# Modulation sums of four vectors in one total on 32 partitions each, read out by one selector product

## The chip, the cores and the metric

One Trainium2 chip, one of its cores. The metric is device time in microseconds (us) of one execution of the whole kernel; the number given is the median of several executions.

## The reference, cut to what matters

Two transformer blocks run on a sequence of 256 positions of width 1024, batch 1, all in fp32. The first has two layers: a convolution mixer and a recurrent/attention mixer, each followed by a gated feed-forward network (FFN) with a 3-tap causal convolution. The second has two layers of FFN, pooling/attention mixer, FFN, each with a modulation that comes from a vector `c` of 1024 numbers:

```python
D_MODEL, SEQ, DEPTH, D_FF, N_SUBLAYERS = 1024, 256, 2, 2816, 3

def modulate(h, shift, scale):
    return h * (1 + scale[:, None, :]) + shift[:, None, :]

# inputs: c (1, 1024); ada_w (2, 1024, 9*1024); ada_b (2, 9*1024)
...
        h = modulate(rms_norm(x, ffn2_norm[l]), sh3, sc3)
        x = x + 0.5 * g3[:, None, :] * swiglu(h, ffn2_w_gate[l], ffn2_w_up[l], ffn2_w_down[l])
```

The nine modulation vectors of a layer (shift, scale and gate of three sublayers, each 1024 wide) are silu(c) @ ada_w[l] + ada_b[l], so there are 18 vectors in the two layers. Each is a product of one row of 1024 with a 1024 x 1024 matrix, 4 MB of weights.

## The kernel before, in words

**Layout.** The activations stand with their 1024 features on 128 partitions in eight tiles. Every weight is split into a high part (ScalarE, line 1078, `wh`) and a low part (VectorE, line 1507, `wl`, the function `lo`), and TensorE multiplies high by high, high by low and low by high. Weights come as units of 1 MB into three slots (`raw`), in one fixed order that SP's queue issues (line 466). A unit's load waits until the split of the unit three places before is done. There are three slots of high and low parts as well.

**An FFN** (ffn0 and ffn1 with convolution, then fa0, fb0, fa1, fb1 without) is eleven blocks of three units: a gate unit, an up unit and, for the block before, a down unit (TensorE lines 666/667 and 768). A block takes TensorE some 17 us. VectorE's part of a block (`part` in its `ffn`) is, in order: the first addition into the gate columns (line 1632), in the convolution FFNs four tap instructions (1641), the split of the next gate unit, the second addition (1654), the product with the activation (1663), the split of the next up unit, the low part of the product (1672, `FX`), the split of the next down unit. Between them ScalarE copies from PSUM (1144, 1169), applies the first tap (1150) and the activation (1164), and makes the high parts (1177). Blocks 2 and later run in a loop of two blocks an iteration; the last ones are written out.

**The modulation sums** run inside five of these FFNs. VectorE does them as multiply-adds: a step takes 128 rows of one vector's matrix (128 x 1024, 512 KB, loaded by one DMA at line 482 into a ring of four slots `ada`), multiplies each row by its number of silu(c), which stands in a column of `CA`, and adds it to the vector's total of 128 x 1024 in `Z` (line 1606; the first step of a vector has no total to add to and is line 1603). A vector needs 8 steps; a block holds four: after the gate split, after the up split, and two after the down split. `ADA_SUMS` says how many vectors an FFN sums: 4, 3, 4, 3, 4 in ffn0, ffn1, fa0, fb0 and fa1, each in its own total and in as many loop iterations as vectors. A load's issue waits until the step four before has been done (`ada_sum`).

**The selector products.** A total still has to be summed over its 128 partitions. `ada_sum_rows` does this on TensorE: for each vector and each half of 512 columns one fp32 product with a 128 x 4 selector from `pick`, whose one column of ones puts the sum into row v of a PSUM bank (line 694). ScalarE copies the four rows out (1098, `ada_take`), TensorE turns them (702, `ada_turn`), VectorE adds the biases (1515, `ada_read`). It happens at five places (`ADA_GAP`): "od" after the fourth unit of the second mixer, in front of its gate matmuls (941, 942) that wait for convolution taps (1944, 1947); "fa0" and "fa1" at the start of these FFNs, in front of the first unit; "w0" and "w1" in the pooling/attention mixers, in front of the q product, whose operand's low part is line 2069.

**Around it.** `angles` is a chain of small VectorE instructions (1749 to 1764) that runs once, in ffn1, before the first addition of block 9. Parameters (gains, biases, taps, `c`) are loaded at the start as rows of `AR` by SP (528, 532), between the first weight units; TensorE turns them in `NPG` groups (882), VectorE copies them out (1816).

## Time and profile before

| | |
|---|---|
| median of 3 executions | 1613.81 us (1613.39 to 1614.95) |
| profiled execution, own time | 1613.69 us |
| its span | 1611.7 us |
| TensorE busy | 1589.0 us (99%) |
| VectorE busy | 1262.0 us (78%) |
| ScalarE busy | 855.1 us (53%) |
| GpSimd busy | 58.6 us (4%) |
| granted TensorE clock, mean | 0.999 |
| HBM read | 341.32 MB |

A line such as `L1606 DVE ...` is line 1606 of the kernel on VectorE; PE is TensorE (PEld its weight loads, PEq its sequencer), ACT ScalarE, POOL GpSimd, SP SyncE, whose work is issuing DMAs. Times in a timeline count from the start of the span. A time in brackets is how long the engine stood idle before the instruction, with the instruction that released it. A matmul's recorded time overlaps the next one's, so matmuls are paced by their starts or by the chain.

### The profile page before, as it was taken

The numbers are of one execution on the slowest core, as the hardware profiler recorded it, in microseconds if no ns is written. First come the engines' busy times: TensorE is split into PE (matmuls) and PEld (weight loads), VectorE is DVE, ScalarE is ACT, GpSimd is POOL, SyncE is SP. The second block draws the span as 40 slices with busy tenths as digits, with TensorE's granted clock in tenths as the row PEclk, the third lists the DMA queues.
The fourth block names the chain that finished last, engine by engine and source line by source line (L and its number), as shares of the span: only waits on it lengthen the run. The fifth ranks groups of instructions, "written<-read, shape, count | busy, mean of one in ns | idle before, by whom it ended". The sixth has DMA issues, their size and how long they took to land.

```text
span 1611.7 us, 26970 instructions
## 1 busy us (share of the span) xinstructions
PE 1589.0 (99%) x11042; PEld 1451.2 (90%) x11044; DVE 1262.0 (78%) x1447; ACT 855.1 (53%) x1025; POOL 58.6 (4%) x76
## 2 busy tenths in 40 slices
PE   9999999999999999999999999999999999999998
PEld 8989999988898999899998899999899998899997
DVE  7978889877678997878878697885878887785555
ACT  6566555555465545644446474445544455564443
POOL 3001000000010000000000010000000000010000
PEclk9999999999999999999999999999999999999999
DMA  9414988644238885498864349875598854265552
GB/s 266 162 53 161 349 300 304 217 158 147 79 119 299 299 290 180 146 325 310 314 216 135 112 158 329 314 243 183 173 324 301 308 167 160 93 196 183 185 194 76
DMA packets 231438, 343.48 MB, mean 213 GB/s; under 512 B 7066, under 2 KB 194048, under 8 KB 231360
## 3 DMA queue, kind: packets, MB, share of 16 engines
q1 hardware_dynamic: 230304, 340.94, 62.4%
q0 software_dynamic: 752, 1.18, 0.2%
q8 instruction: 55, 0.90, 0.2%
q10 hardware_dynamic: 304, 0.27, 0.1%
q14 instruction: 23, 0.19, 0.0%
HBM read 341.32 MB, written 1.05 MB: 212 GB/s over the span
## 4 chain that ended last, share of the span: by engine, by line
PE 80%; DVE 10%; issue 6%; ACT 3%; DMA 0%; DVEq 0%; ACTq 0%
PE PS L666 21%; PE PS L768 19%; PE PS L667 11%; PE PS L657 9%; PE PS L635 5%; PE PS L738 3%; DVE wl L1507 3%; PE PS L644 3%; PE PS L694 2%; PE PS L905 2%; ACT wh L1078 1%; DVE XL L1523 1%; DVE Z L1606 1%; PE PS L832 1%; PE PS L854 1%
## 5 line engine op out<-in xcount | busy, mean ns | idle before, releaser
L1507 DVE TENSOR_TENSOR wl<-raw,wh 128x2048 fp32r<-128x2048 f32 (+2 forms) x256 | 570.1, 2229 | 147.3 <-ACT wh L1078 145.3
L666 PE MATMUL PS<-HP,wh 128*128 128x512 f32 x1728 | 608.0, 395 | 2.1 <-DVE wl L1507 2.1
L1078 ACT ACTIVATE wh<-raw 128x2048 fp32r<-128x2048 f32 (+2 forms) x256 | 475.5, 1859 | 134.0 <-PE PS L768 114.9
L667 PE MATMUL PS<-HP,wl 128*128 128x256 f32 x1728 | 484.6, 280 | 0.0
L666 PEld LDWEIGHTS PS<-HP,wh 128*128 128x128 f32 x1728 | 324.0, 188 | 76.7 <-DVE wl L1507 2.5
L768 PE MATMUL PS<-FX,wh 128*128 128x256 f32 x1920 | 345.0, 281 | 0.4 <-DVE FX L1672 0.4
L667 PEld LDWEIGHTS PS<-HP,wl 128*128 128x128 f32 x1728 | 326.5, 189 | 0.0
L768 PEld LDWEIGHTS PS<-FX,wh 128*128 128x128 f32 x1920 | 294.5, 188 | 2.9 <-issue 0.6
L768 PE MATMUL PS<-FX,wl 128*128 128x256 f32 x960 | 269.9, 281 | 0.0
L768 PEld LDWEIGHTS PS<-FX,wl 128*128 128x128 f32 x960 | 180.4, 188 | 0.0
L1606 DVE SCALAR_TENSOR_TENSOR Z<-ada,CA,Z 128x1024 f32 x126 | 161.4, 1281 | 1.3
L635 PE MATMUL PS<-FX,wh 128*128 128x258 f32 (+2 forms) x592 | 145.0, 285 | 4.7 <-DVE BI L1628 1.8
L635 PE MATMUL PS<-FX,wl 128*128 128x258 f32 (+2 forms) x592 | 143.7, 282 | 0.0
L657 PE MATMUL PS<-HP,wh 128*128 128x256 f32 x768 | 140.9, 285 | 1.2 <-ACT HP L1111 0.6
L1144 ACT ACTIVATE WK<-PS 128x512 f32<-128x512 f32 x54 | 32.3, 598 | 196.8 <-PE PS L667 196.8
L657 PEld LDWEIGHTS PS<-HP,wh 128*128 128x128 f32 x768 | 119.8, 192 | 7.3 <-issue 2.6
L635 PEld LDWEIGHTS PS<-FX,wh 128*128 128x128 f32 (+1 forms) x592 | 111.1, 188 | 8.7 <-DVE BI L1628 2.2
L635 PEld LDWEIGHTS PS<-FX,wl 128*128 128x128 f32 (+1 forms) x592 | 111.2, 188 | 0.0
L657 PE MATMUL PS<-HP,wl 128*128 128x256 f32 x384 | 107.5, 283 | 0.0
L1169 ACT ACTIVATE WK<-PS 128x512 f32<-128x512 f32 x54 | 32.0, 593 | 97.1 <-PE PS L667 97.1
L644 PE MATMUL PS<-XL,wh 128*128 128x256 f32 (+1 forms) x592 | 77.5, 282 | 0.0
L657 PEld LDWEIGHTS PS<-HP,wl 128*128 128x128 f32 x384 | 73.6, 192 | 0.0
(286 smaller groups left out, 1752.7 us busy)
## 6 DMA issues: line engine op xcount, KB each, us to landing
ada<-ada_w SPq DMA_DIRECT2D x144, 512.0 KB, 6.0
raw<-ffn_w_gate SPq DMA_DIRECT2D x66, 1024.0 KB, 5.4
raw<-ffn_w_up SPq DMA_DIRECT2D x66, 1024.0 KB, 5.4
raw<-ffn_w_down SPq DMA_DIRECT2D x66, 1024.0 KB, 5.0
raw<-od_w_in SPq DMA_DIRECT2D x13, 1024.0 KB, 5.3
raw<-ev_w_in SPq DMA_DIRECT2D x10, 1024.0 KB, 8.1
raw<-w_in SPq DMA_DIRECT2D x8, 1024.0 KB, 5.4
raw<-w_out SPq DMA_DIRECT2D x8, 1024.0 KB, 5.8
```

Of the source, the lines that this page charges most:

```text
L635: mm(bank(dst + m, 0, width, slice(0, rows[m])), lhsT=w(a, k, m * P, rows[m]), rhs=XH[:, k, 0:width], start=k == 0 and a == 0, stop=False, ...
L644: last = mm(bank(dst + m, 0, S, slice(0, rows[m])), lhsT=w(0, k, m * P, rows[m]), rhs=XL[:, k, :], start=False, stop=k == KD - 1, skip_gro ...
L657: last = mm(dst, lhsT=lhs(a, k), rhs=rhs(b, k), start=first and i == 0, stop=first and i == len(order) - 1, skip_group_check=not first)
L666: mm(pairs(bank(bk)), lhsT=lhs(0, k), rhs=HP[:, k], start=k == 0, stop=False, skip_group_check=True)
L667: last = mm(bank(bk, 0, S), lhsT=lhs(1, k), rhs=HH[:, k, :], start=False, stop=k == k_tiles - 1, skip_group_check=True)
L694: last = mm(bank(bk + h, 0, 512, slice(0, 4)), lhsT=cn("pick")[:, 3 - v:7 - v], rhs=Z[:, at + v * D + 512 * h:at + v * D + 512 * h + 512], ...
L738: last = mm(bank(bk, m * S, S), lhsT=w(a, k, m * P, P), rhs=H[b][:, k, :], start=m == 0 and k == 0 and i == 0, stop=False, skip_group_chec ...
L768: last = mm(bank(m // 2, (m % 2) * S, S), lhsT=w(a, k, m * P, P), rhs=rhs(b, k), start=begins and i == 0 and m % 2 == 0, stop=False, skip_ ...
L1078: last = A_(dst(wh), src, ACT.Copy)
L1144: A_(pairs(E), PS[:, 4:6, S:], ACT.Copy).then_inc(g_copy, 1)
L1507: last = tt(dst(wl), src, dst(wh).bitcast(F32), ALU.subtract)
L1606: ins = stt(total, w, CA[:, k:k + 1], total, ALU.mult, ALU.add)
```

## The change

Four vectors share one total. Partitions 32i to 32i+31 of the total belong to vector i of the group. A step's slot of `ada` is filled by four DMAs, each 32 rows of one vector's matrix into 32 partitions, so 32 steps sum the four vectors (16 steps sum a group of two, on 64 partitions each). The total is 128 x 1024 for the whole group. VectorE clears it first, and then every step is a multiply-add (the form without a total is gone); its coefficient is a column of `CA`, chosen by a register, which now holds silu(c) in two layouts: 32 columns for 32 rows repeated four times, 16 columns for 64 rows repeated twice. These come from `c` by four and two parameter loads in the place of one, and the parameters fill six groups instead of five. The selector has four columns of ones, one for each quarter (or half), so that one product per half of the columns sums all vectors of the group: two products at each of the five places. The groups are 4, 4, 4, 4 and 2, so ffn1 and fb0 sum four vectors where they summed three, and fa1 two where it summed four. `angles` moves from before block 9 to before block 10 of ffn1, since the loop now covers block 9.

```diff
--- before.py
+++ after.py
@@ -64,7 +64,8 @@
     r.append(("lba", "od_lru_ba", (0,), 4))
     r.append(("lbx", "od_lru_bx", (0,), 4))
     r.append(("lam", "od_lru_lam", (0,), 4))
-    r.append(("c", "c_2", (), 8))
+    r.append(("c4", "c_2", (), 32))
+    r.append(("c2", "c_2", (), 16))
     r.append(("qng", "od_q_norm_g", (0,), 1))
     r.append(("kng", "od_k_norm_g", (0,), 1))
     r.append(("cfw", "ev_cf_conv_w", (0,), 124))
@@ -110,7 +111,7 @@
 def const_layout():
     at = 0
     for name, n in (("ident", P), ("ones", P), ("freq", 1), ("eps", 1), ("mask", 3 * P), ("identb", P // 2), ("heads", 22), ("rot", P),
-                    ("cmask", 2 * P), ("krdup", P), ("krrot", P), ("pick", 7), ("edge", 4 * 16)):
+                    ("cmask", 2 * P), ("krdup", P), ("krrot", P), ("pick", 8), ("edge", 4 * 16)):
         CONST[name] = (at, n)
         at += n
     return at
@@ -167,8 +168,9 @@
     put("edge", e)
     inv = (np.float32(1.0) / np.power(np.float32(10000.0), np.arange(0, 64, 2, dtype=np.float32) / np.float32(64))).astype(np.float32)
     put("freq", np.tile(inv, 4)[:, None])
-    pk = np.zeros((P, 7), np.float32)
-    pk[:, 3] = 1.0
+    pk = np.zeros((P, 8), np.float32)
+    for i in range(P):
+        pk[i, i // 32] = pk[i, 4 + i // 64] = 1.0
     put("pick", pk)
     put("eps", np.full((P, 1), EPS, np.float32))
     return c
@@ -238,8 +240,8 @@
     _n += SUM_PARTS.get(_name, 3)
 
 
-ADA_SUMS = {"ffn0": 4, "ffn1": 3, "fa0": 4, "fb0": 3, "fa1": 4}
-ADA_GAP = {"od": 4, "fa0": 3, "w0": 4, "fa1": 3, "w1": 4}
+ADA_SUMS = {"ffn0": 4, "ffn1": 4, "fa0": 4, "fb0": 4, "fa1": 2}
+ADA_GAP = {"od": 4, "fa0": 4, "w0": 4, "fa1": 4, "w1": 2}
 AC_AT = {"ffn0": 0, "ffn1": 0, "fa0": 1536, "fb0": 0, "fa1": 1536}
 ADA_FROM = dict(zip(ADA_GAP, ADA_SUMS))
 ADA, ADA_AT, _a = {}, {}, 0
@@ -249,7 +251,8 @@
     _a += _k
 assert _a == N_ADA
 
-N_PAR = len(param_rows()) + 2
+COPIES = {"qng": 2, "kng": 2, "c4": 4, "c2": 2}
+N_PAR = sum(COPIES.get(e[0], 1) for e in param_rows())
 TWO_PI = 6.283185307179586
 
 
@@ -301,7 +304,7 @@
         CN = sb("CN", [P, NCONST])
         GM = sb("GM", [P, 6, KD])
         HG = sb("HG", [P, 4, KD])
-        CA = sb("CA", [P, KD])
+        CA = sb("CA", [P, 48])
         SM = sb("SM", [P, 48])
         COS = sb("COS", [P, S])
         SIN = sb("SIN", [P, S])
@@ -472,14 +475,17 @@
                     c = min(256, width - 256 * pair)
                     load(n0 + i, w[:, :, 256 * pair:256 * pair + c], lambda s: s.rearrange("p (k n) -> p k n", k=k))
 
-            aw = A["ada_w_2"].rearrange("l (k p) n -> p l k n", p=P)
-
-            def load_ada(step):
-                g, k = divmod(step, KD)
+            aw = A["ada_w_2"]
+
+            def load_ada(step, at, n):
+
                 if step >= ADA_RING:
-                    sp.wait_ge(ada_sum, step - ADA_RING + 1)
-                l, v = divmod(g, N_ADA // 2)
-                sp.dma_start(ada[:, step % ADA_RING], aw[:, l, k, v * D:(v + 1) * D]).then_inc(ada_in[step % ADA_RING], 16)
+                    sp.wait_ge(ada_sum, step - ADA_RING + 2)
+                for i in range(4):
+                    l, v = divmod(at + i * n // 4, N_ADA // 2)
+                    r = (step - KD * at) * (P // n) + (0 if n == 4 else 32 * (i % 2))
+                    sp.dma_start(ada[32 * i:32 * i + 32, step % ADA_RING],
+                                 aw[l, r:r + 32, v * D:(v + 1) * D]).then_inc(ada_in[step % ADA_RING], 16)
 
             def load_ffn(name, gate, up, down):
                 n0 = U0[name]
@@ -495,7 +501,7 @@
                 def ada_part(j, *ks):
                     if name in ADA_AT and 2 <= j <= 2 * ADA_SUMS[name] + 1:
                         for k in ks:
-                            load_ada(KD * ADA_AT[name] + 4 * (j - 2) + k)
+                            load_ada(KD * ADA_AT[name] + 4 * (j - 2) + k, ADA_AT[name], ADA_SUMS[name])
 
                 wide(n0, gate, 0)
                 wide(n0 + 1, up, 0)
@@ -523,9 +529,10 @@
                 for at in index:
                     v = v[at]
                 dst = AR[r:r + rows, g * P:(g + 1) * P]
-                if name in ("qng", "kng"):
-                    for h in range(2):
-                        sp.dma_start(dst[:, 64 * h:64 * h + 64], v.unsqueeze(0)).then_inc(par_in, 16)
+                if name in COPIES:
+                    m = P // COPIES[name]
+                    for h in range(COPIES[name]):
+                        sp.dma_start(dst[:, m * h:m * h + m], v.rearrange("(t p) -> t p", p=m)).then_inc(par_in, 16)
                     continue
                 if len(v.shape) == 2:
                     v = v.rearrange("k c -> (k c)")
@@ -688,11 +695,11 @@
                 n, at = ADA_GAP[name], AC_AT[ADA_FROM[name]]
                 if ADA[name]:
                     pe.wait_ge(ada_out, ADA[name])
-                pe.wait_ge(ada_sum, KD * (ADA[name] + n))
+                pe.wait_ge(ada_sum, KD * (ADA[name] + n) + 1)
+                pick = cn("pick")[:, 0:4] if n == 4 else cn("pick")[:, 4:8]
                 for h in range(2):
-                    for v in range(n):
-                        last = mm(bank(bk + h, 0, 512, slice(0, 4)), lhsT=cn("pick")[:, 3 - v:7 - v],
-                                  rhs=Z[:, at + v * D + 512 * h:at + v * D + 512 * h + 512], start=v == 0, stop=v == n - 1)
+                    last = mm(bank(bk + h, 0, 512, slice(0, 4)), lhsT=pick, rhs=Z[:, at + 512 * h:at + 512 * h + 512],
+                              start=True, stop=True)
                 last.then_inc(ada_rows, 1)
 
             def ada_turn(name, bk):
@@ -1288,7 +1295,8 @@
             act.wait_ge(ev("ln_var"), 1)
             A_(RT[:, 0:S], bank(7, 0, S), ACT.Sqrt, scale=1.0 / CF, bias=cn("eps")).then_inc(ev("ln_root"), 1)
             act.wait_ge(ev("par_out"), NPG)
-            A_(CA[:], pc("c", 0, 8), ACT.Silu).then_inc(ev("silu_c"), 1)
+            A_(CA[:, 0:32], pc("c4", 0, 32), ACT.Silu).then_inc(ev("silu_c"), 1)
+            A_(CA[:, 32:48], pc("c2", 0, 16), ACT.Silu).then_inc(ev("silu_c"), 1)
             act.wait_ge(ev("ln_normed"), 1)
             for t in range(4):
                 A_(T[:, 4 + t, :], cols(Z, EV["A"], 4)[:, t, :], ACT.Silu, scale=pc("lng", t),
@@ -1594,17 +1602,15 @@
                 lo(n0 + 5)
                 raw_lo(name, 2, gain)
 
-            def ada_step(at, at_z, off, k):
-
+            def ada_step(name, off, k):
+
+                at, at_z, n = ADA_AT[name], AC_AT[name], ADA_SUMS[name]
                 step = KD * at + k
-                dve.wait_ge(ada_in[k % ADA_RING], 16 * (step // ADA_RING + 1) + 16 * (KD // ADA_RING) * off)
-                total, w = Z[:, bass.ds(off * D + at_z, D)], ada[:, k % ADA_RING]
-                if k == 0:
-                    ins = ts(total, w, CA[:, 0:1], None, ALU.mult)
-                else:
-                    dve.wait_ge(ada_sum, KD * off + step)
-                    ins = stt(total, w, CA[:, k:k + 1], total, ALU.mult, ALU.add)
-                ins.then_inc(ada_sum, 1)
+                dve.wait_ge(ada_in[k % ADA_RING], 64 * (step // ADA_RING + 1) + 64 * (KD // ADA_RING) * off)
+                total, w = Z[:, at_z:at_z + D], ada[:, k % ADA_RING]
+                dve.wait_ge(ada_sum, KD * off + step + 1)
+                c = CA[:, bass.ds(KD * off + (0 if n == 4 else 32) + k, 1)]
+                stt(total, w, c, total, ALU.mult, ALU.add).then_inc(ada_sum, 1)
 
             def ffn(f, name, gain, gate=None, chain=None, at_end=None):
                 n0, fb, conv = U0[FFNS[f]], f * NFB, f < 2
@@ -1614,7 +1620,7 @@
                 def part(j, par, ng, nu, nd, off=0, ks=(), mid=None):
                     def ada_some(i):
                         for k in ks[i]:
-                            ada_step(ADA_AT[FFNS[f]], AC_AT[FFNS[f]], off, k)
+                            ada_step(FFNS[f], off, k)
 
                     ks = ks or ((), (), ())
                     C = WK[:, par * 512:(par + 1) * 512]
@@ -1683,11 +1689,17 @@
                 part(1, 1, n0 + 2, n0 + 3, n0 + 4)
                 steps = [((4 * b,), (4 * b + 1,), (4 * b + 2, 4 * b + 3)) if sums else () for b in range(2)]
                 n = sums or 3
+                if sums:
+                    zero = dve.memset(Z[:, AC_AT[FFNS[f]]:AC_AT[FFNS[f]] + D], 0.0)
+                    if f == 0:
+                        zero.then_inc(ada_sum, 1)
+                    else:
+                        own.link(zero)
                 with dve.Fori(0, n) as i:
                     for b in range(2):
                         part(2 * i + (2 + b), b, n0 + 5 + 3 * b, n0 + 6 + 3 * b, n0 + 7 + 3 * b, i, steps[b])
                 for j in range(2 * n + 2, NFB):
-                    if f == 1 and j == 9:
+                    if f == 1 and j == 10:
                         angles()
                     part(j, j % 2, n0 - 1 + 3 * j, n0 + 3 * j, n0 + 1 + 3 * j if j + 1 < NFB else None)
                 if at_end is not None:
@@ -1913,7 +1925,7 @@
             ffnn0, mixn1, ffnn1 = lambda t: pc("ffnn0", t), lambda t: pc("mixn1", t), lambda t: pc("ffnn1", t)
             out_units(U0["ev_out"], "ffn0", ffnn0)
             chain = norm("ffn0", ffnn0, deferred=U0["ffn0"] + 2)
-            dve.wait_ge(ev("silu_c"), 1)
+            dve.wait_ge(ev("silu_c"), 2)
             ffn(0, "mix1", mixn1, chain=chain)
```

## Rows read from the trace of the kernel before

**Rows 1.** Page, part 1.
```profile
PE 1589.0 (99%) x11042; PEld 1451.2 (90%) x11044; DVE 1262.0 (78%) x1447; ACT 855.1 (53%) x1025; POOL 58.6 (4%) x76
```

**Rows 2.** Groups by line (xcount, busy us, mean ns), then the chain: selector products.
```profile
L694 PE MATMUL PS<-Z,CN 128*4 128x512 f32 x72 | 31.7, 592 | 0.0
...
344.33 6.96 PE PS L694 x16
```

**Rows 3.** Timeline, VectorE, od gap (start us, us, instruction).
```profile
348.83 3.25 DVE L1947 SCALAR_TENSOR_TENSOR T<-Z,PR,T 128x256 f32<-128x256 f32 x8
```

**Rows 4.** Timeline, ScalarE, fa0 gap ([idle before <-releaser]).
```profile
657.01 1.02 ACT L1098 ACTIVATE AR<-PS 4x1024 f32<-4x1024 f32 x1 [2.34 <-PE PS L694]
```

**Rows 5.** Timeline, VectorE and TensorE, w0 gap.
```profile
882.45 1.49 DVE L2069 TENSOR_TENSOR HP<-Z,HP 128x1280 fp32r<-128x1280 f32 x1 [1.34 <-ACT HP L1430]
...
893.26 2.29 DVE L1507 TENSOR_TENSOR wl<-raw,wh 128x2048 fp32r<-128x2048 f32 x1 [2.82 <-ACT wh L1078]
...
902.72 2.05 PE L832 MATMUL PS<-Z 128*128 128x128 f32 x16 [0.35 <-DVE Z L2102]
```

**Rows 6.** Timeline of ffn0, then down units of fb1 in the chain.
```profile
165.85 0.69 DVE L1632 TENSOR_TENSOR WK<-PS,WK 128x512 f32<-128x512 f32 x1 [0.31 <-ACT WK L1144]
...
178.51 2.29 DVE L1507 TENSOR_TENSOR wl<-raw,wh 128x2048 fp32r<-128x2048 f32 x1 [0.43 <-ACT wh L1078]
...
234.87 0.68 DVE L1632 TENSOR_TENSOR WK<-PS,WK 128x512 f32<-128x512 f32 x1
...
303.35 0.68 DVE L1632 TENSOR_TENSOR WK<-PS,WK 128x512 f32<-128x512 f32 x1
...
312.24 0.47 PE L768 MATMUL PS<-FX,wh 128*128 128x256 f32 x2 [0.44 <-DVE FX L1672]
...
1456.71 5.76 PE PS L768 x48
...
1490.54 5.76 PE PS L768 x48
```

**Rows 7.** VectorE: groups by line, then timeline (memset; fa0).
```profile
L1606 DVE SCALAR_TENSOR_TENSOR Z<-ada,CA,Z 128x1024 f32 x126 | 161.4, 1281 | 1.3
...
L1603 DVE TENSOR_SCALAR Z<-ada,CA 128x1024 f32 x18 | 13.5, 748 | 0.0
...
329.59 0.27 DVE L1923 MEMSET RS<- 128x256 f32 x1
...
729.94 2.29 DVE L1507 TENSOR_TENSOR wl<-raw,wh 128x2048 fp32r<-128x2048 f32 x1 [0.80 <-ACT wh L1078]
```

**Rows 8.** Timeline, VectorE, ffn1, then its last down units in the chain.
```profile
603.59 0.68 DVE L1632 TENSOR_TENSOR WK<-PS,WK 128x512 f32<-128x512 f32 x1
...
616.66 0.28 DVE L1749 CAST WK<-SIN 128x256 f32<-128x256 int32 x1
...
621.39 0.69 DVE L1632 TENSOR_TENSOR WK<-PS,WK 128x512 f32<-128x512 f32 x1
...
640.52 11.21 PE PS L768 x96
```

**Rows 9.** DMA in ffn0 (40 slices), issues with landing, timeline of fa0.
```profile
GB/s 386 414 357 58 19 0 0 0 0 108 96 248 361 376 390 386 405 424 386 371 268 219 304 373 381 369 359 427 369 417 405 395 424 395 424 414 405 405 424 415
...
raw<-ffn_w_up SPq DMA_DIRECT2D x66, 1024.0 KB, 5.4
...
720.88 0.38 SPq L466 DMA_DIRECT2D raw<-ffn_w_up  x1
...
733.57 1.91 ACT L1078 ACTIVATE wh<-raw 128x2048 fp32r<-128x2048 f32 x1
```

**Rows 10.** Table by stretch: us, busy by engine, granted clock, DMA, GB/s.
```profile
1607.00:1608.00 1.00, 0.00 (x0) 0.00 (x0) 0.96 (x3) 1.00 (x3) 0.00 (x0) 0.77 0.00 0
```

**Rows 11.** Timeline, VectorE, even mixer.
```profile
77.23 2.29 DVE L1507 TENSOR_TENSOR wl<-raw,wh 128x2048 fp32r<-128x2048 f32 x1 [2.59 <-ACT wh L1078]
```

**Rows 12.** DMA rate, 10 to 27 us in 40 slices.
```profile
GB/s 347 349 347 347 352 345 345 352 345 352 349 347 350 367 384 446 395 338 268 300 330 279 265 349 406 294 182 159 149 147 122 127 172 222 253 287 294 311 277 241
```

## The prediction

> **What bounds the kernel now.** I read the page first: TensorE is busy 99% of the span, VectorE 78% [rows 1]. A saving counts only if TensorE really reaches its next work sooner; a delay counts once it reaches TensorE. The groups of instructions and the chain give the work that the change removes: 72 records of the selector products, two to a product, in five places, of which one stands [rows 2]. Third come the timelines around these places, to see what waits there already, and the two paces of a feed-forward (FFN) block. TensorE alone needs 33.83 us for two blocks (1456.71 to 1490.54), but in ffn0 the first additions of blocks 6 and 10 are 68.48 us apart (234.87 to 303.35), 34.24 for two blocks, with no idle time before them: that is VectorE's own cycle [rows 6]. VectorE falls behind there by 0.4 us per two blocks, and at the end of ffn0 TensorE already waits 0.44 us for it. Last comes DMA: in one block with sums it rests for only about 3.4 us of 17 [rows 9].
>
> **Selector products, by place.** A product takes 0.87 us (16 records in 6.96 us), so the five places fall from 8, 6, 8, 6 and 8 products to 2 each: 26 x 0.87 = 22.6 us of TensorE work gone. Only part of it is path.
> - od: the next matmul needs convolution taps that VectorE ends between 350.9 and 352.1, four tiles at 0.4 us each; TensorE came at 351.3 [rows 2, 3]. It now comes 5.2 us earlier and waits: gain 0.3 of 5.2.
> - fa0, fa1: ScalarE had been idle for 2.34 us when the rows came at 657.0, so it takes them as soon as TensorE has them [rows 4]. Nothing else is late: gain 3.4 each.
> - w0, w1: 6 products are 5.2 us, but the low part of the next operand is ready at 883.9, so TensorE arriving at 882.1 waits until 884.0 instead of starting at 887.4: 3.4. VectorE had idled 2.82 us before its split at 893.26; with the high part 3.3 us earlier it is late by the other 0.5, and TensorE waits for VectorE at 902.72 already: 2.9 each [rows 5].
> Sum: 0.3 + 6.8 + 5.8 = **12.9 us gained**.
>
> **VectorE, ffn0.** The first step of each vector becomes a multiply-add: 1.28 for 0.75 us, 0.53 more, once in two blocks. The clear of the total is added; a 256-wide memset is 0.27 us and a 1024-wide tensor_scalar 0.75, so I take 0.72 (bounds 0.27 and 1.28). In ffn0 the clear meets an idle 0.31 before block 2's first addition and the lag an idle 0.43 at 178.5: 0.72 + 0.53 - 0.31 - 0.43 = 0.5 us after the first two blocks, then 3 x 0.53: 2.1 us in all. Nothing absorbs it, as the last down unit already waits [rows 6, 7]: **2.1 us lost**. The register arithmetic moves from the total to the coefficient; I cost it at nothing, as the queue can do it under the instruction before; the tap instructions take a coefficient from a register already.
>
> **VectorE, ffn1.** It goes from three pairs of blocks with sums to four, and the angle chain moves from before block 9 to before block 10. Before, blocks 8 to 10 without sums let VectorE recover. After, the first addition of block 10 comes at 603.59 + 1.56 (lag) + 34.24 + 0.53 + 4.73 (angles: 616.66 to 621.39) = 644.65 us. ffn0 shows 8.89 us from that addition to the last down unit (303.35 to 312.24), so 653.5; TensorE is free for it at 646.1 (640.52 plus half of 11.21): **7.4 us lost** [rows 6, 8]. Queued behind the angles are the last block's additions, taps, the split of the last unit and the product that TensorE needs.
>
> fb0 gets eight steps more and fa1 sixteen fewer; without convolution VectorE idles 0.80 us before a split [rows 7], and 0.53 fits: nothing.
>
> **Clock.** At the end of the kernel TensorE has no work left, and in 1607 to 1608 the granted clock averages 0.77: it falls there from 2.4 to 1.2 GHz [rows 10]. A wait of 7 us would see that too. Its price lies between nothing and a down unit at 1.2 GHz throughout, 5.6 us; I take 1, as one short stretch is hit.
>
> **Start.** Five more parameter loads stand on SP's queue before a weight load, at no more than the 0.38 us of a weight load's issue, 1.9 us; VectorE idles 2.59 us at 77 us, which takes that up [rows 9, 11]. One transpose more: 0.1 us.
>
> **The loads.** Each 512 KB load becomes four, each into 32 partitions. SP issues four where it issued one, at 0.38 us or less each, 1.5 us; its next weight load waits for a split 4 us and more later: hidden. The transfer itself is what the trace doesn't show. While data flows in a block with sums (204 to 221 us), it moves about 395 GB/s; the 5.24 MB of a block need 13.3 us, 5.3 of them for the 2.10 MB of the vectors [rows 9]. One bound is that narrow loads cost the same, or less. The nearest row for loads into few partitions is the start, where the small parameter loads run: 122 to 182 GB/s between 21 and 25 us, against 345 to 352 with wide ones [rows 12]; their packets are also small, so it is the outer bound (0.4 of the rate). I take half the rate, between the two but nearer to the only narrow row: 10.6 us for the vectors, 18.6 for the block. The block lasts 17.4 with convolution, 16.9 without. The queue lags by 1.2 and 1.7 us per block, plus 1.7 at once, as a down unit with two vector loads outlasts its gap. Against it stands the lead of the weights: an up unit issued at 720.88 lands 5.4 us later and is read at 733.57, 7.3 after that [rows 9]; I take the same for the convolution FFNs. Over 8 blocks: 9.6 + 1.7 - 7.3 = 4.0 us twice (ffn0, ffn1) and 13.6 + 1.7 - 7.3 = 8.0 twice (fa0, fb0); fa1 has 4 blocks and stays within its lead. **24.0 us lost** (bounds 0 and, at 0.4 of the rate, where a block takes 21.2 us and fa1 stalls too, about 119).
> The Trainium skill (SBUF — State Buffer, Door 1: The DMA port swizzle) says that a load's bandwidth depends on how many of 16 ports its partitions reach, and that 32 neighbouring partitions reach 8. By it the vectors' loads run at half rate, which is also my figure; by its advice to use one load over all partitions the change is the wrong way round. No row here shows it.
>
> **Sum.** 1613.7 (the profiled execution's own time, 2.0 over its span and 0.1 under the median) - 12.9 + 2.1 + 7.4 + 1.0 + 0.1 + 24.0 = 1635.4, say **1635 us**.
>
> **Rivals.**
> - A, not slower: the narrow loads stay hidden. For it: DMA rests 3.4 us a block, and small packets alone may explain the start's rate. Then 1611.4; it decides at a flow for the vectors above about 230 GB/s, where the block takes 17.1 us. Between 1609 and 1614. Chance 0.33.
> - B, all of the selector products pay: fillers can be taken away where other work is ready. The rows at od and w0 speak against it. With the loads hidden and VectorE's lag absorbed: 1613.7 - 22.6 + 0.7 = about 1592. Chance 0.04.
> - C, the loads are worse than half: each small load also pays its own start and landing. At a block of 19.5 us the same sums give 2 x 11.2, 2 x 15.2 and 4.8 in fa1, 57.6 us: 1669, and more beyond. Chance 0.08.
> - The forecast: 0.55, since the only rows with narrow loads show a much lower rate.
>
> **Numbers.** The range leaves out B, most of C and little of A: 1610 to 1665; the likeliest case alone spans 1620 to 1660. A measurement of this kernel can tell about 0.2% (3.2 us) from no change. Slower by more: the forecast and C, 0.62 with a little of A's upper end. Within: most of A, 0.25. Faster by more: A with a free clock, and B, 0.13.
>
> **What would show it.** Right: 20 records of selector products; a wait before the od gate matmuls of about 5 us and one before the q product of about 2; TensorE waiting for FX near the end of ffn0 and, with the angles just before it, of ffn1; DMA shares of 1 without gaps in blocks with sums, weights landing after 6 us and more, ScalarE's high parts waiting for DMA from the fourth block on, TensorE's stalls growing towards the end of ffn0, ffn1, fa0 and fb0 and none in fa1. Wrong: rests in the DMA row of a block with sums, a landing near 6 us and two blocks of fa0 in 33.8 us mean rival A; TensorE without a wait after the selector products means B.

## The result and the profile after

The kernel after takes **1743.2 us** (median of 4 runs, 1732.9 to 1754.5), the kernel before 1614.3 in the same measurement: a ratio of 1.080, with an interval of 1.073 to 1.087. The prediction said 1635 with a range of 1610 to 1665. It had the sign and the place, and it had the size wrong by a factor of six (21 us of loss against 129). All rows of after are from one profiled execution of 1732.9 us, the fastest of the four. The versions with narrow loads scatter by 1 to 2% from one execution to the next where the kernel before stays within 0.1%, so I read no difference of less than some 10 us between them.

The page, part 1, a page line on the packets, and one of the groups of instructions:

```profile
PE 1608.4 (93%) x10991; PEld 1470.8 (85%) x10993; DVE 1274.5 (74%) x1453; ACT 854.7 (49%) x1026; POOL 58.1 (3%) x76
...
DMA packets 238594, 343.56 MB, mean 198 GB/s; under 512 B 14226, under 2 KB 201200, under 8 KB 238512
```

```profile
L701 PE MATMUL PS<-Z,CN 128*4 128x512 f32 x20 | 9.4, 592 | 0.0
```

TensorE no longer fills the span: it is busy for 93% of it, against 99% [rows 1]. The 72 records of the selector products [rows 2] have become 20, as the change intends. What it lost stands in the timeline of TensorE: first the waits inside fa0 and at its end, then the ends of ffn0 and ffn1, the od gap [rows 3] and the w0 gap [rows 5].

```profile
826.48 0.50 PE L673 MATMUL PS<-HP,wh 128*128 128x512 f32 x1 [1.54 <-DVE wl L1515]
...
847.43 0.50 PE L673 MATMUL PS<-HP,wh 128*128 128x512 f32 x1 [1.92 <-DVE wl L1515]
868.34 0.50 PE L673 MATMUL PS<-HP,wh 128*128 128x512 f32 x1 [1.88 <-DVE wl L1515]
...
934.34 0.76 PE L775 MATMUL PS<-FX,wh 128*128 128x256 f32 x2 [4.74 <-DVE FX L1678]
...
339.81 0.77 PE L775 MATMUL PS<-FX,wh 128*128 128x256 f32 x2 [4.77 <-DVE FX L1678]
379.96 1.19 PE L948 MATMUL PS<-T,PW 128*128 128x256 f32 x2 [4.89 <-DVE T L1959]
...
715.48 0.77 PE L775 MATMUL PS<-FX,wh 128*128 128x256 f32 x2 [10.07 <-DVE FX L1678]
...
979.63 0.47 PE L664 MATMUL PS<-HP,wh 128*128 128x256 f32 x2 [1.86 <-DVE HP L2081]
```

A block of fa0 now lasts 20.9 us (847.43 to 868.34) where it lasted 16.91. TensorE is held up by VectorE's low parts, those by ScalarE's high parts, and those by the weights. The chain of work that ended last shows the whole circle in one block (start, us, what; "..." stands for pieces of 0.02 us without a releaser):

```profile
826.45 16.66 DMA raw<-ffn_w_gate
...
843.14 1.92 ACT wh L1085
...
845.08 2.30 DVE wl L1515
...
847.40 16.62 DMA raw<-ffn_w_gate
```

The gate weights of a block are issued when a split has freed their buffer, land 16.66 us later, are split in 1.92 and 2.30 us, and that split frees the buffer for the next. An up unit used to land after 5.4 us [rows 9]. The table by stretch says what fills the 16.66 us (us, busy by engine, granted clock, DMA share, GB/s), and the issues say that the loads of a block are late, the weights' too (count, KB, median us to landing):

```profile
826.45:847.40 20.95, 17.84 (x112) 15.60 (x112) 14.24 (x12) 7.75 (x7) 0.00 (x0) 1.00 1.07 251
```

```profile
ada<-ada_w SPq DMA_DIRECT2D x576, 128.0 KB, 9.5
raw<-ffn_w_gate SPq DMA_DIRECT2D x66, 1024.0 KB, 11.3
raw<-ffn_w_up SPq DMA_DIRECT2D x66, 1024.0 KB, 10.2
raw<-od_w_in SPq DMA_DIRECT2D x13, 1024.0 KB, 5.4
```

The share is full (1.07) while only 250 GB/s flow. DMA is busy all the time with slow packets. The records of the packets agree. Over the whole execution a packet of 4096 bytes (a row of a vector's load or of a down unit) took 159 ns in the median before and 252 ns after. Inside fa0 both kinds of load are slower by about the same factor: between 738.6 and 772.5 us of the kernel before (two blocks) the mean was 178 ns for 4096 bytes and 51 for 1024 (gate and up weights), between 826.5 and 868.3 us of the kernel after it was 257 and 77. All packets of a block keep 16 DMA engines busy for 15.1 us before and for 22.4 after. Loads of stages without vectors (od_w_in, 5.4 us) are as before.

SP's queue is held up as well. Four small loads took their issues 7.29 and 5.54 us here, and the up unit's load stands behind them:

```profile
827.65 7.29 SPq L487 DMA_DIRECT2D ada<-ada_w  x4
834.99 0.42 SPq L469 DMA_DIRECT2D raw<-ffn_w_up  x1
835.45 5.54 SPq L487 DMA_DIRECT2D ada<-ada_w  x4
```

For the account I cut the executions at nine reciprocals of norms (a 128x256 reciprocal on VectorE each), which all versions have. The last two columns are the changes of `a_spread4` and `a_pool_fill`, described below, and "none" means within 0.1 us.

| stage (us) | before | after | change | spread, elements | spread, filled |
|---|---|---|---|---|---|
| start to ffn0's norm | 135.11 | 136.50 | +1.4 | +8.0 | +1.6 |
| ffn0 | 192.62 | 220.16 | +27.5 | +3.4 | +3.4 |
| od | 141.85 | 144.44 | +2.6 | +2.1 | none |
| ffn1, fa0's product | 194.14 | 231.08 | +36.9 | +8.3 | +2.5 |
| fa0 | 190.29 | 217.36 | +27.1 | none | none |
| w0, w0's product | 92.11 | 89.02 | -3.1 | -1.7 | -3.1 |
| fb0, fa1's product | 193.42 | 223.53 | +30.1 | -3.65 | -3.7 |
| fa1 | 190.30 | 190.30 | none | none | none |
| w1, w1's product | 92.13 | 89.03 | -3.1 | -1.8 | -3.1 |
| fb1 and the end | 189.7 | 189.7 | none | none | none |

The changes of after add up to 119.4 us, the difference of the two spans (the medians differ by 129). The four FFNs with 32 steps of sums hold more than all of it (121.6); fa1, with 16 steps of sums instead of 32, lost nothing.

### The profile page after: what moved, and what is told of

Read it like the earlier page. It is cut to its first block, busy times and chain, and to the rows that moved or that the text cites. A ratio compares the mean times of both kernels' runs of the same rounds, so it can differ in the third digit from the quotient of the medians.

```text
span 1731.1 us, 27468 instructions
## 1 busy us (share of the span) xinstructions
PE 1608.4 (93%) x10991; PEld 1470.8 (85%) x10993; DVE 1274.5 (74%) x1453; ACT 854.7 (49%) x1026; POOL 58.1 (3%) x76
## 2 busy tenths in 40 slices
DMA packets 238594, 343.56 MB, mean 198 GB/s; under 512 B 14226, under 2 KB 201200, under 8 KB 238512
## 4 chain that ended last, share of the span: by engine, by line
PE 45%; DMA 25%; DVE 15%; ACT 6%; issue 5%; SPq 4%; DVEq 0%; ACTq 0%
DMA raw<-ffn_w_gate 13%; PE PS L775 10%; PE PS L673 8%; PE PS L664 7%; DMA ada<-ada_w 6%; DVE wl L1515 6%; PE PS L642 5%; SPq L487 4%; PE PS L674 4%; ACT wh L1085 4%; DMA raw<-ffn_w_down 4%; PE PS L745 3%; PE PS L651 2%; DMA raw<-ffn_w_up 2%; DVE Z L1613 2%
## 5 line engine op out<-in xcount | busy, mean ns | idle before, releaser
L673 PE MATMUL PS<-HP,wh 128*128 128x512 f32 x1728 | 627.7, 405 | 57.4 <-DVE wl L1515 57.4
L674 PE MATMUL PS<-HP,wl 128*128 128x256 f32 x1728 | 491.5, 284 | 0.0
L673 PEld LDWEIGHTS PS<-HP,wh 128*128 128x128 f32 x1728 | 332.2, 192 | 142.4 <-DVE wl L1515 53.4
L775 PE MATMUL PS<-FX,wh 128*128 128x256 f32 x1920 | 355.2, 287 | 35.9 <-DVE FX L1678 24.8
L775 PEld LDWEIGHTS PS<-FX,wh 128*128 128x128 f32 x1920 | 301.9, 193 | 44.2 <-issue 30.9
L674 PEld LDWEIGHTS PS<-HP,wl 128*128 128x128 f32 x1728 | 334.4, 194 | 0.0
L1613 DVE SCALAR_TENSOR_TENSOR Z<-ada,CA,Z 128x1024 f32<-128x1024 f32 x144 | 184.3, 1280 | 5.1
L775 PEld LDWEIGHTS PS<-FX,wl 128*128 128x128 f32 x960 | 185.1, 193 | 0.0
L664 PEld LDWEIGHTS PS<-HP,wh 128*128 128x128 f32 x768 | 120.9, 193 | 10.9 <-issue 8.1
L664 PE MATMUL PS<-HP,wl 128*128 128x256 f32 x384 | 108.0, 284 | 0.0
L664 PEld LDWEIGHTS PS<-HP,wl 128*128 128x128 f32 x384 | 74.1, 193 | 0.0
L651 PEld LDWEIGHTS PS<-XL,wh 128*128 128x128 f32 (+1 forms) x592 | 73.0, 186 | 0.5
L1151 ACT ACTIVATE WK<-PS 128x512 f32<-128x512 f32 x54 | 31.8, 588 | 83.1 <-PE PS L674 83.1
```

What stands on the lines that cost most here:

```text
L651: last = mm(bank(dst + m, 0, S, slice(0, rows[m])), lhsT=w(0, k, m * P, rows[m]), rhs=XL[:, k, :], start=False, stop=k == KD - 1, skip_gro ...
L664: last = mm(dst, lhsT=lhs(a, k), rhs=rhs(b, k), start=first and i == 0, stop=first and i == len(order) - 1, skip_group_check=not first)
L673: mm(pairs(bank(bk)), lhsT=lhs(0, k), rhs=HP[:, k], start=k == 0, stop=False, skip_group_check=True)
L674: last = mm(bank(bk, 0, S), lhsT=lhs(1, k), rhs=HH[:, k, :], start=False, stop=k == k_tiles - 1, skip_group_check=True)
L775: last = mm(bank(m // 2, (m % 2) * S, S), lhsT=w(a, k, m * P, P), rhs=rhs(b, k), start=begins and i == 0 and m % 2 == 0, stop=False, skip_ ...
L1151: A_(pairs(E), PS[:, 4:6, S:], ACT.Copy).then_inc(g_copy, 1)
```

## The experiments

The edits are shortened to their main lines.

Two theories could make the loads slow. **Width**: packets into few neighbouring partitions get in each other's way. **Count**: four DMAs where there was one cost SP's queue and the DMA engines four starts and four ends. A third, **VectorE**, says that the loads are not the cause.

### The loads alone, narrow and spread

`b_narrow4` is the kernel before with the loads of the change:

```diff
-sp.dma_start(ada[:, slot], aw[:, l, k, v * D:(v + 1) * D])
+for q in range(4):
+    sp.dma_start(ada[32*q:32*q+32, slot], aw[32*q:32*q+32, l, k, v * D:(v + 1) * D])
```

> The kernel before, with one edit: each vector load of 512 KB is split into four DMAs of 128 KB, each into 32 neighbouring partitions; sums, selector products and the place of the angles stay. If the loads are all of the loss (width or count of the DMAs alike): 1614 plus 131 (1743 less the 1612 that the other terms give) = about 1745 us. If the loss sits in the new sums, the angles or the wait for the products: about 1614 to 1625.

Measured: 1738.4 us, ratio 1.080 (1.074 to 1.086). The loads alone cost as much as the whole change. By stage they cost 30.5 us in ffn0 and 26.8 in fa0, and in fa1, which still has 32 steps here, 21.4; in ffn1 and fb0, with 24 steps, 12.1 and 15.3. `b_spread4` differs from it in the partitions, and in the rows of the source that go with them:

```diff
-    sp.dma_start(ada[32*q:32*q+32, slot], aw[32*q:32*q+32, l, k, v * D:(v + 1) * D])
+    sp.dma_start(ada[q::4, slot], aw[q::4, l, k, v * D:(v + 1) * D])
```

> The kernel before, with each vector load split into four DMAs of 128 KB, each into 32 partitions that lie four apart (0, 4, 8, ...; 1, 5, 9, ...). As many DMAs, packets and bytes as in the narrow split, only the partitions differ. Theory width (a packet takes longer where many packets go into few neighbouring partitions): packets of 4096 bytes back near 159 ns, 1614 to 1625 us. Theory count (four issues of 0.46 us on SP's queue and the small closing packets of each DMA): about 1745, as the narrow split.

Measured: 1613.9 us, ratio 1.0001 (0.9991 to 1.0011): no loss at all. Both have 6912 packets under 512 B more than before, 16 for each of 432 more DMAs. The count costs nothing, the place of the 32 partitions everything; that the other source rows do not matter is shown by `a_spread4` below, which reads the same rows as the kernel after. The packet line is word for word the same but for the rate; here of narrow, then of spread, each with its issues:

```profile
DMA packets 238354, 343.54 MB, mean 200 GB/s; under 512 B 13978, under 2 KB 200960, under 8 KB 238272
...
ada<-ada_w SPq DMA_DIRECT2D x576, 128.0 KB, 9.2
raw<-ffn_w_gate SPq DMA_DIRECT2D x66, 1024.0 KB, 9.5
```

```profile
DMA packets 238354, 343.54 MB, mean 213 GB/s; under 512 B 13978, under 2 KB 200960, under 8 KB 238272
...
ada<-ada_w SPq DMA_DIRECT2D x576, 128.0 KB, 4.4
raw<-ffn_w_gate SPq DMA_DIRECT2D x66, 1024.0 KB, 5.5
```

### Which partitions meet

`a_alternate` is the kernel after with its four small loads in another order:

```diff
-for i in range(4):
+for i in (0, 2, 1, 3):
```

> The kernel after, with the four small loads of a step in the order of partitions 0, 64, 32, 96 instead of 0, 32, 64, 96. Theory width, where the loads into 0 to 31 and 32 to 63 share one half of the ways into SBUF, as the port table says, and consecutive loads overlap: two loads in flight use both halves, so much of the loss goes: 1640 to 1700 us. Theory width of each load alone: no change, 1743 within its spread of some 10 us. Theory count: no change either, 1743.

Measured: 1687.3 us, ratio 1.047 (1.044 to 1.050). The same four loads in another order give back 56 of 129 us, which neither the count nor the width of each load alone can do. The median of the 4096-byte packets falls with it, from 252 to 233 ns. `b_half2` widens the loads to 64 partitions:

```diff
-sp.dma_start(ada[:, slot], aw[:, l, k, v * D:(v + 1) * D])
+for q in range(2):
+    sp.dma_start(ada[64*q:64*q+64, slot], aw[64*q:64*q+64, l, k, v * D:(v + 1) * D])
```

> The kernel before, with each vector load split into two DMAs of 256 KB, into partitions 0 to 63 and 64 to 127. Theory of the halves (partitions 0 to 63 share one half of the ways into SBUF, as the port table says): two of every two packets in flight meet as in the narrow split, so nearly all of its loss: 1700 to 1740 us. Theory of the plain width (64 partitions have twice the ways of 32): little or no loss, 1614 to 1640.

Measured: 1746.4 us, ratio 1.085 (1.080 to 1.090). Loads into 64 neighbouring partitions are as slow as into 32. `b_half2` and the orders 0, 32, 64, 96 have in common that the queue changes between the halves 0 to 63 and 64 to 127 after every 256 KB; in `a_alternate` it does so after every 128 KB, and more of the loads that overlap lie in different halves. The four runs fit two sets of ways into SBUF, one for each half. The Trainium skill (SBUF — State Buffer, Door 1: The DMA port swizzle) says just this: 0 to 31 and 0 to 63 both reach 8 of 16 ports. The slow runs of 32 and of 64 neighbours agree with it, and so does the full speed of partitions that lie four apart.

### One load per step

`a_wide` fills the 128 partitions of a step in one DMA, with the four vectors as the source's outermost dimension:

```diff
-for i in range(4):
-    sp.dma_start(ada[32 * i:32 * i + 32, slot], aw[l, r:r + 32, v * D:(v + 1) * D])
+sp.dma_start(ada[:, slot], aw[l, r:r + 32, v * D:(v + 4) * D].rearrange("r (v d) -> v r d", v=4))
```

> The kernel after, with the 128 partitions of a step filled by one DMA of 512 KB instead of four of 128 KB (two DMAs, of 32 and 96 partitions, in fa0, whose four vectors cross from one layer to the next). Same values in the same places. If the loads are all of the loss beyond the other terms: 1611 to 1613 us, with waits of about 5 us before the od gate matmuls, 2 before each q product, 2 at the end of ffn0 and 7 at the end of ffn1. If VectorE's part of the loss is larger than the 9.5 us that the prediction gave it: above 1620.

Measured: 2220.7 us, ratio 1.378 (1.375 to 1.381). A miss, and a second trap. Its waits (us in total, times, longest), a stretch of ffn0 (columns as in the table by stretch above) and its packets:

```profile
DVE Z L1618 <- DMA ada<-ada_w: 378.7, 142, 10.0
...
PE PS L676 <- DVE wl L1518: 315.0, 62, 16.7
```

```profile
200.00:240.00 40.00, 24.40 (x123) 21.48 (x124) 22.69 (x23) 12.84 (x14) 0.00 (x0) 0.79 0.54 172
```

```profile
DMA packets 230400, 343.51 MB, mean 155 GB/s; under 512 B 6035, under 2 KB 193009, under 8 KB 230321
```

After has 14226 packets under 512 B, 576 x 16 = 9216 of them the closing ones of the vectors' loads, so 5010 others. Here 1025 are left for the vectors' 176 loads, and the sizes of the outermost dimension give 96 x 4 + 16 x 2 + 32 x 16 + 32 x 3 = 1024. A load thus ran on as many DMA engines as its outermost dimension has entries, mostly 4. The Trainium skill has this rule (DMA: Bandwidth & Descriptors, Why a DMA increments its semaphore by 16 and not by 1: the slowest dimension's size decides how many engines take part), and the number of packets agrees with it. It is another trap than the first: the DMA engines are busy for only 0.54 of that stretch, not 1.07, and the 4096-byte packets are back at 159 ns in the median. As the experiment says nothing on the VectorE part, the same holds of its sister with the angles moved to od (the edit is below):

> The one-load version of the kernel after, with the ten angle instructions moved from before block 10 of ffn1 to the end of the attention of od, where VectorE waits 7.91 us for ScalarE (row at 449.77 of the kernel before). If the angles before block 10 cost what the prediction says: 7.4 us less than the one-load version, about 1604. If the end of ffn1 is late for another reason: as the one-load version.

Measured: 2211.0 us, ratio 1.370 (1.365 to 1.374), 9.7 less, between versions of which each scatters by 15 us: no more than a hint.

### The change without narrow loads

`a_spread4` is the kernel after with vector i on partitions i, i + 4, ...:

```diff
-    sp.dma_start(ada[32 * i:32 * i + 32, slot], ...)
+    sp.dma_start(ada[i::4, slot], ...)
-    pk[i, i // 32] = pk[i, 4 + i // 64] = 1.0
+    pk[i, i % 4] = pk[i, 4 + i % 4 // 2] = 1.0
-    sp.dma_start(dst[:, m * h:m * h + m], v.rearrange("(t p) -> t p", p=m))
+    sp.dma_start(dst[:, h::4], v.rearrange("(t p) -> t p", p=m)[:, o:o + 32])
```

> The kernel after, with vector i of a step on partitions i, i + 4, i + 8, ... instead of 32 neighbouring ones; selectors and the coefficients in that order (the coefficients' parameter loads at the start now write single elements of 4 bytes, 8 loads in place of 6). Still four DMAs of 128 KB. If the width is all of the loss beyond the other terms: 1611 us, up to 1616 if the element loads at the start delay the first units (6144 packets more, 9 ns each in the kernel before, on 16 DMA engines: 3.5 us). If VectorE's part is larger than the 9.5 us that the prediction gave it: above 1620.

Measured: 1626.5 us, ratio 1.008 (1.007 to 1.010). The source rows are those of the kernel after, and the 4096-byte packets are back at 159 ns. The narrow loads cost the rest, 117 us and more, as this version has a slower start of its own. But 13 us of loss remain where my other terms gave a gain of 2.3. TensorE's waits in it:

```profile
PE PS L782 <- DVE FX L1685: 10.5, 2, 7.7
PE PS L896 <- issue: 5.3, 1, 5.3
PE PS L955 <- DVE T L1966: 4.9, 1, 4.9
PE PS L671 <- DVE HP L2088: 3.7, 2, 1.9
```

These are the ends of ffn0 and ffn1 (2.8 and 7.7), the start (my own edit: the parameters' transposes wait for the single-element loads), the od gap and the two w gaps. They are the waits that the prediction named, with its sizes. What it did not have is the clock behind them. The table by stretch around the od gap (us, busy of TensorE, its weight loads, VectorE, ScalarE and GpSimd, granted clock, DMA share, GB/s):

```profile
360.00:362.00 2.00, 0.00 (x0) 0.00 (x0) 2.00 (x6) 0.00 (x0) 0.00 (x0) 0.60 0.24 32
362.00:364.00 2.00, 1.54 (x4) 1.30 (x5) 2.00 (x5) 0.00 (x0) 0.00 (x0) 0.50 0.98 329
364.00:366.00 2.00, 2.00 (x7) 1.55 (x5) 1.70 (x1) 0.84 (x2) 0.00 (x0) 0.50 0.47 163
366.00:368.00 2.00, 2.00 (x14) 2.00 (x13) 0.00 (x0) 0.84 (x2) 0.00 (x0) 0.70 0.48 114
```

TensorE had been idle for 4.9 us, and the clock is at 0.50, the level of 1.2 GHz, for the four us in which it works again (in the kernel before it is 1.00 throughout). So od, with 0.3 us to gain, loses 2.1. Three more runs part the angles and the form of the load. In the first the angles move:

```diff
-if f == 1 and j == 10:
-    angles()
+angles()      # in od, ahead of the last fill of the attention; its buffers change with the place
```

> The same, with the angles moved from before block 10 of ffn1 to the end of the attention of od, where they cost nothing in the kernel before (1613.9 us both ways). If the angles before block 10 cost what the prediction says: 7.4 us less than with them there, about 1604. If the end of ffn1 is late for another reason: no difference.

Measured: 1621.4 us, ratio 1.004 (1.003 to 1.006): 5.2 less, not 7.4. TensorE's wait at the end of ffn1 falls from 7.7 to 2.8 us and does not go: those 2.8 are the lag of the sums, as at the end of ffn0. The control is the same move in the kernel before:

> The kernel before, with the angle instructions moved from before block 9 of ffn1 to the end of the attention of od. If the angles cost nothing in the kernel before (VectorE catches up in blocks 9 and 10): 1613 to 1615 us. If they already cost something there: 1606 to 1612.

Measured: 1613.9 us, ratio 1.000 (0.999 to 1.001). The angles cost nothing before, and 5.2 us before block 10 of the changed ffn1. Third, one DMA per step with the rows outermost, the rest as in `a_spread4_od`:

```diff
+sp.dma_start(ada[:, slot], aw[l, r:r + 32, v * D:(v + 4) * D].rearrange("r (v d) -> r v d", v=4))
```

> The same again, with one DMA of 512 KB per step where the four vectors lie side by side (ffn0, ffn1, fb0), its source's outermost dimension the 32 rows. Theory: the one-load version took 2220 us because its source's outermost dimension was the 4 vectors and only as many DMA engines took part (4 closing packets per DMA instead of 16). Then this one runs on 16 and gives the time of the four spread loads, within 2 us. If one load with a source of three dimensions is slow in itself: over 1800.

Measured: 1620.6 us, ratio 1.005 (1.003 to 1.006), the time of four spread loads. It has 4607 packets under 512 B fewer than with four loads, about 48 for each of the 96 steps with one load: 16 closing packets where there were 64, so these loads ran on 16 engines. With the 32 rows outermost the one load is as good, so the engine count was what held `a_wide` up. (The order of the partitions differs between the two as well, but the packets of `a_wide` were not slow.)

### The clock and the start

`b_od2` makes one wait in the kernel before, by leaving out three of the four vectors at od, whose values are then missing:

```diff
-for v in range(n):
+for v in range(1 if name == "od" else n):
```

> The kernel before, with 2 selector products at od in place of 8 (three of the four vectors are left out there); nothing else changes. TensorE then waits 5 us for the taps. The prediction's term: 0.3 us gained, 1613.2. Clock theory (a wait of 5 us makes the granted clock fall to 1.2 GHz in the stretch behind it, as the windows behind the od wait of the spread version show): TensorE's next 4 to 5 us run slower and nothing takes that up, 2 us lost, about 1616.

Measured: 1615.8 us against 1613.8, ratio 1.0012 (1.0003 to 1.0021): six products fewer, and 2 us slower (in the profiled execution the stage od takes 1.4 us more, the span 1.9). Its wait is 4.9 us as predicted, and the stretch behind it again at half clock (columns as above; before shows 1.00 and 14 records in 352 to 354):

```profile
348.00:350.00 2.00, 0.00 (x0) 0.00 (x0) 2.00 (x4) 0.00 (x0) 0.00 (x0) 1.00 0.39 131
350.00:352.00 2.00, 0.70 (x2) 0.64 (x3) 2.00 (x6) 0.00 (x0) 0.00 (x0) 0.82 0.75 204
352.00:354.00 2.00, 2.00 (x7) 1.55 (x6) 2.00 (x2) 0.56 (x2) 0.00 (x0) 0.50 0.90 320
354.00:356.00 2.00, 2.00 (x14) 1.88 (x13) 0.54 (x1) 1.12 (x3) 0.00 (x0) 0.83 0.17 15
```

`a_pool_od` is `a_spread4_od` with the coefficients loaded in whole rows, two small loads in place of eight, and put in order by three copies on GpSimd:

```diff
+sp.dma_start(CR[r:r + rows, 0:m], v.rearrange("(t p) -> t p", p=m))
+pool.tensor_copy(AR[0:32, 0:P].rearrange("t (q i) -> t q i", i=4), CR[0:32, 0:32].unsqueeze(2).to_broadcast([32, 32, 4]))
```

> The spread version with the angles in od, and the coefficients of the two layouts now loaded once, as 2 small loads of whole rows, and spread over the partitions' order by three copies on GpSimd, in place of 8 loads of single elements. The element loads cost 8 us at the start (first norm's reciprocal of ev's output at 114.3 us instead of 106.3, of which 5.3 are TensorE's wait before the parameters' transposes). If that is so: 1621.4 - 7 to 8 = about 1614. If the start's loss has another cause (more parameters as such): above 1619.

Measured: 1612.9 us, ratio 0.9997 (0.9988 to 1.0006): 8.5 less, 8.2 of it at the start by the traces (ffn0's norm at 135.3 us, not 143.5). `a_pool_fill` keeps TensorE busy in the gaps, by giving the same product again:

```diff
-for h in range(2):
+for h in [0, 1] * {"od": 4, "w0": 2, "w1": 2}.get(name, 1):
```

> The same, with the selector products given again where TensorE otherwise waits: 8 at od as in the kernel before, 4 at w0 and w1, 2 at fa0 and fa1 (the same product written again to the same place). Clock theory: od no longer loses its 2.1 us and w0, w1 each gain up to 1.1 more, so 2 to 4 us less than without: about 1611. If the waits cost only their own time: no difference, as TensorE would have waited there.

Measured: 1610.3 us, ratio 0.9976 (0.9967 to 0.9985), the only version that is faster than before, by 3.6 us. It gives ten products more than `a_pool_od`, six at od and two each at w0 and w1, and is 2.6 us faster. Nearly all of that is the stage od, with its six: 144.3 us without them, 141.8 with them (the starts of the two profiled executions differ by 1.4 us the other way, so their spans by less than the medians). At w0 and w1 the two versions are equal (89.0 us): there TensorE's gap of 1.9 us did not bring the clock down in `a_pool_od`, though it did in `a_spread4` (stages of 90.4 us). The waits at the ends of ffn0 and ffn1 remain in the filled version (2.77 and 2.99 us), and the second has its slow stretch too:

```profile
655.17 0.47 PE L788 MATMUL PS<-FX,wh 128*128 128x256 f32 x2 [2.99 <-DVE FX L1692]
```

```profile
656.00:660.00 4.00, 4.00 (x24) 4.00 (x23) 3.09 (x3) 3.45 (x8) 0.00 (x0) 0.57 0.32 97
```

## Why the prediction was wrong, point by point

- **The loads: the step that failed.** The prediction gave the narrow bytes half the rate (10.6 us of a block's 18.6), left the weights' bytes at the full rate (8.0 us), and got 24.0 us, 4.0 twice and 8.0 twice. The sign and the threshold were right; this term was too small by a factor of almost five. Measured, with the spread version's other losses taken off by stage: 24.1 in ffn0 (27.5 - 3.4), 28.6 in ffn1, 27.1 in fa0, 33.8 in fb0, together 113.6. What the runs show in place of the step is that the whole block slows down, not its narrow bytes alone: 250 GB/s instead of 395, 20.9 us for 5.24 MB, the weights' 1024-byte packets at 77 ns instead of 51, as much slower as those of 4096 bytes. Put on the vectors alone, that is 12.9 us for their 2.10 MB, 163 GB/s or 0.41 of 395. Why wide packets beside narrow ones slow down as much is argued only: they need the same ways.
- **The size of the error.** The error in a block's time is an eighth, but the loss is what lies above a threshold: at 18.6 us a block is 1.7 over TensorE's 16.9 and the lead of 7.3 pays for half of that; at 20.9 it is 4.0 over, and the same lead pays for a quarter. A smaller slip points the same way: the prediction took 17.4 us for a block with convolution, but its own row has 68.48 us for four, 17.1. With that, half the rate would have given 6.2 in ffn0 and in ffn1 instead of 4.0.
- **The outer bound** (0.4 of the rate, a block of 21.2, about 119 us) came close, from the start's row [rows 12], the only one with narrow loads, which the prediction then moved away from because its packets are small. Part of that is luck. No run here says whether width or small packets made that row slow, and the bound holds 11.6 us for fa1, which lost nothing; without it, it is 107 against 113.6.
- **fa1** was said to stay within its lead, with 4 blocks of sums, and it did (190.3 us both ways), but not for the reason given: by the prediction's own sum a block of 20.9 costs 10 us there. The trace shows that the lead lasts longer. In fa0 TensorE keeps its pace of 17 us a block until 807 us, over two blocks after the first step of the sums at 766.8. In fa1 VectorE's blocks with late loads last 19.6 us twice and the next 11.0, so it catches up before TensorE needs it. With 32 steps in fa1 (`b_narrow4`) the stage loses 21.4 us. Why fb0 loses more than fa0, with blocks of 22.2 us at 237 to 240 GB/s, stays open.
- **SP's issues** were called hidden, at 1.5 us for four. In two blocks of fa0 of `b_spread4` four take 2.4 to 3.7 us and are hidden indeed, as nothing is lost. In the kernel after they are not: four take up to 7.3 us, and a weight load waits behind them. As the same number of issues costs nothing with spread partitions, this follows from the narrow loads; how much of their price goes through SP's queue was not measured.
- **The products.** 20 records; fa1 gains 3.65 (3.4 predicted), w0 and w1 3.1 each (2.9): right. od waits 4.9 us as predicted, and still the term is wrong: not 0.3 gained but 1.4 (`b_od2`) to 2.6 (after) lost in that stage, by the clock.
- **VectorE.** The clear took 0.91 us (0.72 taken). In the spread version the last unit of ffn0 waits 2.77 us, 2.3 more than before (2.1 predicted), that of ffn1 7.7 (7.4 predicted). Right, but each is followed by slow TensorE work: the stage of ffn1 lost 12.0 us once the 3.65 gained at fa0's product are added back to its 8.3.
- **The clock: too small.** The prediction charged 1 us, for one stretch. Behind every wait of 2.8 us or more `a_spread4` shows one: about 1 us in ffn0, 2.4 in od, 4 in ffn1, 2.7 at the start behind my element loads. These are differences between a stage's loss and its wait, so small waits of other kinds are in them; only od's was measured by itself (`b_od2`, `a_pool_fill`).
- **The rivals.** Rival A, hidden loads, would not have been 1611: the spread version without its element loads' 6.6 us stands at 1620, 0.4% slower. Rival C (a block of 19.5 us, 1669 us and beyond) was the right direction with a chance of 0.08; the outer bound belonged in it, with more than that. Its mechanism, each small load paying its own start and landing, is refuted by `b_spread4`.

That loads in flight together slow each other, and not only each one by itself, is shown by `a_alternate`, which changes nothing but the order. Which partitions share a way was measured only as far as these runs go: 32 neighbours, 64 neighbours, and every fourth. The rest is argued from the port table of the Trainium skill that is named above.

## What to carry to other kernels

Price a load by the partitions that it writes and by the outermost dimension of its source, not by its bytes: the same 128 KB loads cost nothing on every fourth partition and 8% of this kernel on 32 neighbours, and the version with 512 KB loads on 4 DMA engines was 38% slower, against 0.5% with 16 engines. Charge the slow load to its neighbours in the queue too: here the weights' packets took 1.5 times as long. Where a term hangs on a threshold (a block just over TensorE's time), carry both ends of its rate through to the end of the sum before choosing, and give the far end its weight. Work taken from TensorE just ahead of something it must wait for saves only what the wait leaves over (3.1 of 5.2 us at w0, nothing at od), and can cost: find what it waits for next. At od it paid to leave the work in.

## What was not expected of the hardware

- Loads into 64 neighbouring partitions (ratio 1.085) are no better than into 32 (1.080), while 32 partitions that lie four apart are as good as 128 (1.0001).
- The order of four loads in one queue is worth 56 us: 0, 64, 32, 96 against 0, 32, 64, 96.
- Ten useless matmul products make the kernel 2.6 us faster (1612.9 to 1610.3), by the six of them at od, 5.2 us of TensorE work; taking six away there in the kernel before makes it 2.0 us slower.
- Narrow loads slow the wide ones beside them by as much as themselves (1024-byte packets 51 to 77 ns, 4096-byte packets 178 to 257 ns in a block of fa0).
- Some 6000 packets of one 4-byte element each, off the steady part of the kernel, cost 6.6 to 8.5 us at the start.
